# A fused ten-stage network in fp32 halves: the first four weight slots of each norm's stage are multiplied with x times the norm's weight, and the inverse root is multiplied in afterwards

## What is computed

```python
def rmsnorm(x, g):
    y = x * rsqrt(mean(x * x, axis=-1) + EPS)
    return y * g

for layer in range(2):
    p = split_columns(rmsnorm(x, norm_g[layer]) @ w_in[layer])    # 74 slots of weights
    x = x + branches(p) @ w_out[layer]                            # 16 slots
x = x + 0.5 * swiglu(rmsnorm(x, ffn1_norm), gate, up, down)       # 66 slots
n = rmsnorm(x, mix_norm)
x = x + merged(n @ w_in, sigmoid(n @ w_gate + b_gate)) @ w_out    # 52 slots
x = x + 0.5 * swiglu(rmsnorm(x, ffn2_norm), gate2, up2, down2)    # 66 slots
return rmsnorm(x, final_norm)
```

## Time and profile before

| | us |
|---|---|
| median of 3 executions | 1348.96 (1344.74 to 1351.25) |
| profiled execution, span from first to last instruction | 1335.5 |
| TensorE busy, products | 1233.7 (92%) |
| VectorE busy | 847.5 (63%) |
| GpSimd busy | 662.6 (50%) |
| ScalarE busy | 651.5 (49%) |

### The profile page before, as it was taken

One profiled execution on the slowest core, in us unless ns is written; L12 is line 12 of the kernel. 1 busy time (PEld: TensorE's weight loads), 2 busy tenths in 40 slices (PEclk: granted clock), 3 DMA queues, 4 the chain that ended last, 5 costly groups with the idle time before them and its releaser, 6 DMA issues.

```text
span 1335.5 us, 25358 instructions
## 1 busy us (share of the span) xinstructions
PE 1233.7 (92%) x9388; PEld 1161.2 (87%) x9388; DVE 847.5 (63%) x1199; ACT 651.5 (49%) x1019; POOL 662.6 (50%) x317
## 2 busy tenths in 40 slices
PE   7988987999989989879999999999899899999997
PEld 6976886998889868769989899999878789899997
DVE  5659988687844599885978532222357748555553
ACT  5642565445556425653454544444556345444442
POOL 3434446464535444463545455555454345555551
PEclk9988998999979889989999899999899889899998
DMA  6533224452634322344526555556344345465651
GB/s 207 190 104 100 90 96 155 149 179 92 221 118 152 110 102 81 102 155 135 182 96 218 168 191 188 190 197 194 127 152 133 113 140 191 137 193 189 195 196 48
DMA packets 57286, 199.54 MB, mean 149 GB/s; under 512 B 6352, under 2 KB 9456, under 8 KB 57072
## 3 DMA queue, kind: packets, MB, share of 16 engines
q1 hardware_dynamic: 53520, 193.95, 44.3%
q10 hardware_dynamic: 3680, 4.42, 1.1%
HBM read 196.52 MB, written 1.84 MB: 149 GB/s over the span
## 4 chain that ended last, share of the span: by engine, by line
PE 62%; DVE 23%; issue 7%; ACT 5%; DMA 2%; POOL 1%; ACTq 0%; DVEq 0%; SPq 0%; POOLq 0%
PE ps L1298 36%; PE ps L1318 15%; DVE ca L1014 3%; PE ps L1308 3%; DVE ring L740 2%; ACT ring L371 2%; PE ps L1282 2%; DVE y L1054 1%; DVE gs L926 1%; DMA raw<-in_w 1%; DVE qke L941 1%; PE ps L1414 1%; DVE gat L959 1%; DVE rms L730 1%; PE ps L1538 1%
## 5 line engine op out<-in xcount | busy, mean ns | idle before, releaser
L254 POOL TENSOR_TENSOR ring<-raw,ring 128x1024 fp32r<-128x1024 f32 x242 | 592.8, 2453 | 557.7 <-ACT ring L371 557.5
L1298 PE MATMUL ps<-xs,ring 128*128 128x256 f32 x5760 | 712.1, 285 | 24.4 <-ACT xs L385 7.9
L1298 PEld LDWEIGHTS ps<-xs,ring 128*128 128x128 f32 x5760 | 691.0, 194 | 42.7 <-issue 16.5
L371 ACT ACTIVATE ring<-raw 128x1024 fp32r<-128x1024 f32 x364 | 383.1, 1054 | 204.7 <-DMA raw<-in_w 65.9
L740 DVE TENSOR_TENSOR ring<-raw,ring 128x1024 fp32r<-128x1024 f32 x122 | 154.8, 1269 | 205.3 <-ACT ring L371 203.9
L1318 PE MATMUL ps<-ys,ring 128*128 128x256 f32 x2016 | 241.9, 280 | 7.7 <-DVE ys L771 7.2
L1318 PEld LDWEIGHTS ps<-ys,ring 128*128 128x128 f32 x2016 | 236.9, 190 | 8.6 <-DVE ys L771 6.6
L1308 PE MATMUL ps<-ring,xs 128*128 128x512 f32 x480 | 131.3, 430 | 8.1 <-ACT ca L435 8.1
L1308 PEld LDWEIGHTS ps<-ring,xs 128*128 128x128 f32 x480 | 96.9, 207 | 32.3 <-issue 10.5
L1014 DVE SCALAR_TENSOR_TENSOR ca<-conv,par,ca 128x256 f32<-128x256 f32 x96 | 80.8, 848 | 12.8 <-ACT ca L435 11.3
L771 DVE TENSOR_TENSOR ys<-ca,ys 128x256 fp32r<-128x256 f32 x44 | 59.6, 1355 | 22.8 <-ACT ys L611 22.8
(11 more groups left out here) (246 smaller groups left out, 1076.9 us busy)
## 6 DMA issues: line engine op xcount, KB each, us to landing
raw<-in_w SPq DMA_DIRECT2D x364, 512.0 KB, 3.3
y<-bias_rows ACTq DMA_DIRECT2D x6, 256.0 KB, 3.1
x<-in_x SPq DMA_DIRECT2D x1, 1024.0 KB, 7.8
out_y<-y SPq DMA_DIRECT2D x4, 256.0 KB, 2.3
const<-in_const SPq DMA_DIRECT2D x1, 896.0 KB, 11.9
bias_rows<-lg ACTq DMA_DIRECT2D x1, 768.0 KB, 5.9
par<-in_par ACTq DMA_DIRECT2D x3, 181.0 KB, 2.5
dec<-in_wT ACTq DMA_DIRECT2D x1, 512.0 KB, 3.7
```

The source lines that it names most:

```text
L254: pool.tensor_tensor(ring[:, g % RING, 1, :], raw[:, g % RAW, :], ring[:, g % RING, 0, :].bitcast(F32), ALU.subtract).then_inc(lo[g % RAW], 1)
L371: act.activation(ring[:, g % RING, 0, :], raw[:, g % RAW, :], ACT.Copy).then_inc(S["hi"], 1)
L1298: last = mm(ps[bank][:, half * T:(half + 1) * T], ring[:, slot % RING, wp, (at + k) * P:(at + k + 1) * P], rhs(k, xp), start=(i == 0), sto ...
```

## The change

A constant `EARLY = 4` is added. The first four slots of each of the five stages work on x times the norm's weight, without the root. Their results are multiplied by the root when VectorE takes them out of PSUM (`times_factor`), and the rest of the stage works on the normed x as before.

ScalarE writes the high parts of x times weight behind `update_x` (`early`), VectorE all 8 low parts (`early_lo`). The sum of squares is now ones times squares, 8 products of 256 columns into bank 4, so that every partition has the sum; it stands behind slot 0 in TensorE's order. The root is Ln and Exp on 128x256, the refining step too is 128x256. VectorE writes x times root (`normed`, four of 128x512), ScalarE the high parts of that times weight once slot 3 has read the tile (`xs_free`), VectorE all low parts (`norm_lo`). The diagonals, the spread product and GpSimd's low parts (`norm_odd`) go. In the feed-forward parts the first two hidden tiles read the scaled copies in `ex[:, 2:4]`. The gate jobs in the layers move from slots 0 to 2 to slots 4 and 5, x is loaded in four pieces, and at the start the bias copies come ahead of the splits. The final norm uses the new root, and takes its factor from SBUF instead of PSUM.

```diff
@@ SyncE
-            sp.dma_start(x[:], d["x"]).then_inc(S["x_in"], 16)
+            for c in range(N_UPDATES):
+                sp.dma_start(x[:, 2 * c:2 * c + 2, :], d["x"][:, 2 * c:2 * c + 2, :]).then_inc(x_in[c], 16)
@@ ScalarE
+            def early(n, g, col):
+                for k in range(KT):
...
+                    act.activation(xs[:, k, 0, :], x[:, k, :], ACT.Identity, scale=g[:, col + k:col + k + 1])\
+                        .then_inc(S["u_hi"], 1)
+            def factor(n):
+                inverse_root(n, var[:, 0:T], rms[:, 0:T], S["var0"], n + 1, S["rms0"])
+            def norm(n, g, col, used):
+                for k in range(KT):
+                    act.wait_ge(S["x_f"], n * (KT // 2) + (k // 2 + 1))
+                    if k < KT - 1:
+                        act.wait_ge(S["xs_free"], n * (KT - 1) + (k + 1))
+                    else:
+                        act.wait_ge(S["slots_used"], used)
+                    act.activation(xs[:, k, 0, :], xn[:, k, :], ACT.Identity, scale=g[:, col + k:col + k + 1])\
+                        .then_inc(S["x_hi"], 1)
@@ ScalarE, layers
+                split(0, it, LAYER_SLOTS)
+                factor(it)
+                for p in range(1, EARLY):
+                    split(p, it, LAYER_SLOTS)
+                for r in range(EARLY):
+                    evacuate(r)
+                norm(it, gains, V_G, it * LAYER_SLOTS + EARLY)
+                for p in range(EARLY, IN_SLOTS):
...
+                early(it + 1, par, V_G)
                 squares(it + 1)
                 split(LAYER_SLOTS - 1, it, LAYER_SLOTS)
-                norm(it + 1)
@@ ScalarE, feed-forward
+                act.wait_ge(S["slots_used"], at + 1)
+                split(at)
+                factor(n)
+                early_gate(0)
+                split(at + 1)
+                early_hi(0)
+                split(at + 2)
+                norm(n, g, col, at + EARLY)
+                early_gate(1)
+                split(at + 3)
+                early_hi(1)
+                split(at + 4)
@@ VectorE
+            def early_lo(n, g, col):
+                for k in range(KT):
+                    dve.wait_ge(S["u_hi"], n * KT + (k + 1))
+                    stt(xs[:, k, 1, :], x[:, k, :], g[:, col + k:col + k + 1], xs[:, k, 0, :].bitcast(F32),
+                        ALU.mult, ALU.subtract).then_inc(S["u_lo"], 1)
+            def factor(n):
                 dve.wait_ge(S["ssq"], n + 1)
+                mean_square(var[:, 0:T], ps[4][:, 0:T], D, S["var0"])
                 dve.wait_ge(S["rms0"], n + 1)
+                refine(var[:, 0:T], rms[:, 0:T])
+            def times_factor(dst, bank, scale):
+                n = dst.shape[0]
+                return stt(dst, ps[bank][0:n, 0:T], -0.5 * scale, rms[0:n, 0:T], ALU.mult, ALU.mult)\
+                    .then_inc(S["early"], 1)
+            def normed(pair):
+                r = rms[:, 0:T].rearrange("p (o t) -> p o t", o=1).broadcast_to((P, 2, T))
+                tt(xn[:, 2 * pair:2 * pair + 2, :], x[:, 2 * pair:2 * pair + 2, :], r, ALU.mult)\
+                    .then_inc(S["x_f"], 1)
+            def norm_lo(n, g, col):
+                for k in range(KT):
                     dve.wait_ge(S["x_hi"], n * KT + (k + 1))
+                    stt(xs[:, k, 1, :], xn[:, k, :], g[:, col + k:col + k + 1], xs[:, k, 0, :].bitcast(F32),
+                        ALU.mult, ALU.subtract).then_inc(S["x_lo"], 1)
@@ VectorE, layers (the mixer alike)
+                split(0, it, LAYER_SLOTS)
+                factor(it)
+                times_factor(rows[0:104, :], 0, 1.0)
+                dve.wait_ge(S["slots_used"], it * LAYER_SLOTS + 2)
+                times_factor(ik[:], 1, 1.0)
+                for r in range(R_IQ, EARLY):
+                    dve.wait_ge(S["slots_used"], it * LAYER_SLOTS + (r + 1))
+                    times_factor(iq[:, r - R_IQ, :], r, 0.125)
+                for c in range(N_UPDATES):
+                    normed(c)
+                norm_lo(it, gains, V_G)
+                for p in range(1, IN_SLOTS):
@@ VectorE, feed-forward
+                split(at)
+                factor(n)
+                early_gate(0)
+                early_up(0)
+                for c in range(N_UPDATES):
+                    normed(c)
+                split(at + 1)
+                split(at + 2)
+                norm_lo(n, gains if n == 2 else gains2, V_G if n == 2 else col)
+                early_gate(1)
+                early_up(1)
+                split(at + 3)
+                split(at + 4)
@@ TensorE
                 for k in range(KT):
                     if k % 2 == 0:
                         pe.wait_ge(S["sq"], n * 4 + k // 2 + 1)
-                    for tt in range(2):
-                        last = mm(ps[0][:, tt:tt + 1], sqs[:, k * T + tt * P:k * T + (tt + 1) * P], ones[:, 0:1],
-                                  start=(k == 0 and tt == 0), stop=(k == KT - 1), skip_group_check=True)
+                    last = mm(ps[4][:, 0:T], ones, sqs[:, k * T:(k + 1) * T], start=(k == 0), stop=(k == KT - 1))
                 last.then_inc(S["ssq"], 1)
-                pe.wait_ge(S["diag"], n + 1)
-                mm(ps[1][:, 0:T], ones, diag, start=True, stop=True).then_inc(S["spread"], 1)
@@ TensorE, feed-forward
+                for r in range(EARLY):
+                    here(at + r)
+                    tile_product(r, 0, at + r, xs_part, ready=early_ready(n) if r == 0 else None,
+                                 freed=(r == EARLY - 1)).then_inc(S["slots_used"], 1)
+                    if r == 0:
+                        sum_squares(n)
                 pe.wait_ge(S["y_lo"], y_done + 1)
                 here(at + 4)
                 sum_slot(at + 4, 0, True, False)
+                pe.wait_ge(S["x_hi"], n * KT + KT)
+                pe.wait_ge(S["x_lo"], n * KT + KT)
```

232 lines of the change are left out of this document (125 added, 107 removed).

## The result

The changed kernel takes 1355.62 us in the median of 17 executions (1347.69 to 1365.42), the kernel before 1344.74 in 17 beside it (1337.7 to 1356.35): a ratio of 1.009, with an interval from 1.0065 to 1.0115. It is slower: the medians are 10.9 us apart, and the ratio is worth 12. The forecast was 1365, slower. Of the distance of 9.4 us, 4.2 us is its base (the median of three executions was 1348.96, that of 17 is 1344.74), the rest its sum: + 16.6 where the two profiled executions are 10.4 apart.

A forecast was written before the change was run, and what follows sets the result against it. TensorE, busy 92% of 1335.5 us, was taken as the bound, with time lost or won only at six norms. Terms summed to + 16.6 us on 1348.96, giving 1365.6, taken as 1365; range 1340 to 1380.

The forecast's parts named there:

- The bound and the mechanism: TensorE bounds the kernel, time changes only at six norms; the gap moves from ahead of slot 0 to slot 4.
- E: At each norm, the end of TensorE's last product before it; the forecast counts its times from there.
- Rival A: Collisions do not fall as placed and the clock holds: - 0.2 us in all, 1349; chance 0.2.
- Rival B: Tail behind slot 3 hidden too, leaving slot 0, squares and full pace: - 19 us, 1330; chance 0.15 with its half.
- late gates at 0: Layers: gates starting later cost 0; if their cover is gone, 1 to 3 us per layer.
- Rival C: Longer tail: trickling slots drop the clock (+ 1.7 three times), late gates cost 2 us per layer; + 25, 1374; chance 0.2.
- at the mark: At each norm, a point behind which the old pace runs on: slot 4's end, or slot 5's start in feed-forward parts.
- layer 0: Start of the kernel: slot 4 ends at 44.2 against 38.2 us, one block of 2.4 included; + 6.0.
- layer 1: Layer 1's norm: mark at E + 26.6, 0.8 us faster, given back by a slow clock after the jump; 0.
- ffn 1: First feed-forward norm: collisions with GpSimd's splits put slot 5 at E + 27.1 against 24.6; + 2.5.
- clock + 2.3: Each feed-forward norm: after the gap the loop starts at half speed for 3.5 to 6 us; 2.3 us each.
- list of signs of being wrong: Slot 4 without a gap, 8 squares' products much under 3.8 us, or new VectorE operations at 0.4 to 0.7 throughout.

The follow-up runs named there:

- e8: Changed kernel with the feed-forward parts' splits of slots 1 and 2 put directly behind the norm; 1343.76 us, ratio 0.998 to the kernel before.
- e2: Changed kernel; layers and mix: x times root ahead of the last factors, ScalarE's splits of slots 1 to 3 behind the norm; 1367.48 us, ratio 1.0148.
- c0_changed: The changed kernel run once more without any edit, as a mark for the others; 1353.43 us, ratio 1.0063 to the kernel before.
- e6: Changed kernel with the first weight slot split ahead of the early parts of x at the start; ratio 1.0101 to the kernel before.
- e9: e8 with the root put ahead of the split of each stage's first slot, on ScalarE and VectorE; ratio 1.0036 to the kernel before.
- e11: The edits of e6 and e9 in one kernel, feed-forward stages as in e8; one execution, 1346.89 us, beside 1338.62 of the kernel before.
- e4: Changed kernel with ten products of constants added on TensorE in both feed-forward gaps; ratio 1.0065 to the kernel before.
- e3: Changed kernel with both engines' splits of slots 1 to 4 in the feed-forward parts behind the norm and second hidden tile; ratio 1.0053.
- e8_again: The kernel of e8 unchanged, run again in more rounds; 1350.10 us, ratio 1.0031 to the kernel before.
- e10_mix: e8 with, in the mix, x times root ahead of the last factors and splits between norm and last evacuations; 1347.13 us, ratio 0.9994.

## Why the prediction was right, and where its terms were off

**The bound and the mechanism held.** TensorE without a gap from E to about E + 17 (E + 20 in one of two traces of layer 1), the gap behind slot 3, VectorE at 2.2 us where GpSimd splits, half clock behind the feed-forward gaps: all there. That GpSimd's splits are a cause and not neighbours is shown by e8: the same operations without a split beside them take 0.42 and 2.49 us, and the two feed-forward parts, each at the faster pace, are together 5 to 8 us shorter. Rival A (no collisions, the clock holds) is excluded for the changed kernel, and is about what e8 makes of it. Rival B did not come: the tail can be hidden in the layers (e2), but with this order the gates lose their cover and are later themselves. An order that hides the tail and leaves the gates where they were was not run, so B stays open for another kernel. The lost cover is the condition that the prediction gave for its "late gates at 0". Rival C was right in part: the clock did drop behind the gaps of the layers and the mix, but that cost less than C's 1.7 us three times, and the gates were covered.

**The terms**, forecast and measured, changed less before, each in the changed kernel and then in c0_changed:

| | forecast | at the mark | over the stage |
|---|---|---|---|
| layer 0 | + 6.0 | + 6.6, + 5.7 (gate's columns) | + 4.9, + 5.0 |
| layer 1 | 0 | + 0.9, - 1.6 | - 1.6, - 0.6 |
| ffn 1 | + 2.5, clock + 2.3 | + 1.0, + 0.9, clock + 2.9, + 1.6 | + 3.8, + 2.4 |
| mix | + 0.2 | - 0.4, - 1.0 | + 1.4, + 2.1 |
| ffn 2 | + 1.4, clock + 2.3 | - 0.7, + 0.5, clock + 1.7, + 1.8 | + 1.0, + 2.3 |
| end | + 1.9 | | + 1.0, + 1.0 |
| sum | + 16.6 | | + 10.5, + 12.1 |

The direction rests on layer 0, the two feed-forward parts and the end. The sum was half again too large, its errors have both signs, and that most marks came out within 1.5 us is in part luck.

**Units too dear.** Rows of single instructions were used for rows of eight. The low parts cost 3.25 us for 8 (0.41 each; one alone 0.48), not 3.9; the high parts 3.30 (0.49 alone, 0.48 forecast); the 8 squares' products 3.26 (21.97 to 25.23), not 4.0. That is under the 3.8 that the prediction gave as its lower bound, and on its list of signs of being wrong. The Trainium skill (ScalarE: Activation LUTs, What ACT_TABLE_LOAD costs) says that ScalarE's instructions, back to back, overlap by some 93 ns; the trace agrees, with 0.494 alone and 0.40 from start to start. At a feed-forward norm squares and late low parts make 1.4 of the 1.5 and 2.1 us by which slot 5 came sooner than forecast; the end (1.0 in place of 1.9) is short by its squares and its last 8 operations (3.26 in place of 3.8).

**Terms left out in layer 1.** Its forecast of E + 26.6 lies between the two traces (28.3 and 25.8), and not for its reasons. x times root was not blocked (2.71 us; the forecast had 0.8 more). ScalarE evacuates bank 0 in four instructions ahead of its high parts (404.60 to 406.47), which the prediction called free; VectorE's low parts waited 0.41 us for them. Slot 4 ends 1.4 and 1.8 us behind the last low part (in the mix 0.95) and not 0.15: its last products run at half clock. And the changed kernel's slot 0 took 4.3 us at a granted 0.50 where c0_changed had 2.8 at 1.00; that and TensorE's wait behind the loop's jump (3.49 and 2.11 us) are the difference between the two.

**Right for a wrong reason: layer 0.** The root was counted as hidden by 4 us. It was done at 33.5, just ahead of slot 3's end at 33.9 (in c0_changed at 33.4, behind slot 3's end at 33.0), because its mean was queued behind a split that waited for a load; e6, e9 and e11 show chains of one length where the prediction saw one. The block of x times root that it placed there is real: 5.37 us in place of 2.5.

**The clock** was forecast at 2.3 per feed-forward gap and cost 2.9 or 1.6 (two executions of the first) and 1.7 or 1.8; e4 gives it back by keeping TensorE busy. In the layers and the mix the prediction took nothing for it. It fell there too (last section): from the last low part to slot 7's end TensorE took 0.4 to 1.7 us more than at full clock, within the 1.7 that the prediction left open.

**What the marks left out.** The prediction took a mark's shift as the stage's. Only the feed-forward parts are steady enough to test that: there mark and clock together are + 3.9 and + 2.5 in the first, + 1.0 and + 2.3 in the second, against + 3.8 and + 2.4, + 1.0 and + 2.3 over the stage. For the layers and the mix what an execution varies by is larger than the difference.

## What to carry to other kernels

An operation that leaves the critical path pays only if what it left behind does not gather in front of the next wait: here a gap of 8 us ahead of slot 0 became one of 2 to 5 us ahead of slot 4, plus the work that had been added. When GpSimd and VectorE share the work, place GpSimd's two-operand jobs by time, not by slot order: moving two splits 6 us later (from E + 14.7 to E + 20.3) took more off a stage than every new order of the tail. The splits have to go somewhere, though: in e2 they landed on the gates, in e3 on the loads. And before speeding up one of the chains that meet at a wait, look for the others: if three end within 2 us, an edit of one of them cannot show.

## What the runs showed of the hardware

**TensorE has two paces at full clock.** A loop's 48 products take 5.60 or 5.82 us, with the granted clock at 1.00 and no wait between them. The kernel of e8_mid and e8_again is the same, and it shows both, in swapped stages; rows of TensorE in the first and the second feed-forward part, first in e8_mid, then in e8_again:

```profile
787.26 5.82 PE L1390 MATMUL ps<-xs,ring 128*128 128x256 f32 x48
...
1188.35 5.60 PE L1390 MATMUL ps<-xs,ring 128*128 128x256 f32 x48
```
```profile
788.56 5.60 PE L1390 MATMUL ps<-xs,ring 128*128 128x256 f32 x48
...
1190.74 5.82 PE L1390 MATMUL ps<-xs,ring 128*128 128x256 f32 x48
```

In each of these executions the pace then holds for the rest of the loop, 0.32 us for every three slots, an estimated 6 us over the loop's 20 groups. The stages differ by 4.6 us (195.1 against 190.5 in the first part, 195.8 against 191.2 in the second), as the faster one had a loss of its own each time: half clock in the first, a wait of 1.28 us ahead of slot 0 in the second. The pace changed at waits: in e3_ffn from 5.70 to 5.82 across one of 3.47 us, in e10_mix from 5.82 to 5.60 across one of 0.59. It is no property of a kernel, so a stage may be compared between traces only at one pace, and it is a part of the up to 19 us by which executions of one kernel differ. From start to start a product takes 113 ns at the one and 118 at the other (a slot and sum slot of 72 in 8.16 and 8.48 us). The Trainium skill (TensorE: Matmul & The Clock Gate, Wait — 56ns, not 53.3ns?) has one value for a warm array, the columns at 2.4 GHz and 2.5 ns, an estimated 109 ns for 256; the rows show two, both above it. What chooses the pace stays open.

**The clock** fell to half 4.2 us into a wait of 5.1 us and rose 6.0 us after products had come again. The stretches of the changed kernel at the first feed-forward gap, and behind layer 1's gap ahead of slot 4 (us; busy PE, PEld, DVE, ACT, POOL; granted clock, DMA share, GB/s):

```profile
772.00:774.00 2.00, 0.00 (x0) 0.00 (x0) 2.00 (x5) 2.00 (x6) 0.00 (x0) 1.00 0.69 250
776.00:778.00 2.00, 1.22 (x5) 1.23 (x6) 1.81 (x5) 1.30 (x2) 0.00 (x0) 0.50 0.00 0
780.00:782.00 2.00, 2.00 (x11) 2.00 (x11) 0.14 (x1) 0.00 (x0) 2.00 (x1) 0.50 0.35 84
784.00:786.00 2.00, 2.00 (x20) 2.00 (x19) 0.00 (x0) 0.59 (x1) 2.00 (x1) 1.00 0.57 223
...
408.00:410.00 2.00, 2.00 (x12) 2.00 (x11) 2.00 (x6) 1.79 (x5) 0.00 (x0) 0.50 0.00 0
```

The length of a wait alone does not tell whether the clock falls: it fell at waits of 2.37, 2.67 and 2.97 us ahead of slot 5 (e8_again, e9_root_first, e11_both, first part; 48 products in 7.29, 7.33 and 7.09 us) and held at 2.38 and 2.72 (e3_ffn, first part, and e9_root_first, second part; 5.71 and 5.72).

**Two table loads for each root, still.** The Ln and the Exp of the roots (L350, L351) have 12 loads of 1.283 us each in the changed kernel, for 12 roots (6 of them new with the norms); before, the Exp had 6 for 6. Where the Trainium skill (ScalarE: Activation LUTs, Table sets) would have one load per root, the trace of after disagrees too.
